# Moving the tail of a retention normalisation behind later attention units, on one core

## The reference, cut to what matters

```python
def retention_readout(y, g, gn_gain):
    mu = jnp.mean(y, axis=-1, keepdims=True)
    var = jnp.mean(jnp.square(y - mu), axis=-1, keepdims=True)
    y = (y - mu) * lax.rsqrt(var + EPS)
    y = jnp.swapaxes(y, 1, 2).reshape(y.shape[0], y.shape[2], -1) * gn_gain.astype(jnp.float32)
    return (y * jax.nn.silu(g.astype(jnp.float32))).astype(g.dtype)

def gated_merge(gates, ya, yb, yc, w_ret, w_win, w_na, w_out):
    ga, gb, gc = jnp.split(jax.nn.sigmoid(gates), N_BRANCHES, axis=-1)
    return (ga * (ya @ w_ret) + gb * (yb @ w_win) + gc * (yc @ w_na)) @ w_out
```

## Time and profile before

| what | value |
|---|---|
| median of 3 runs | 1686.57 us (1684.5 to 1687.13) |
| the profiled execution | 1686.03 us |
| its span, first to last instruction | 1684.2 us |
| TensorE matmul busy | 1439.9 us (85%) |
| VectorE busy | 807.2 us (48%) |
| ScalarE busy | 589.8 us (35%) |
| mean granted TensorE clock | 0.921 of full |

### The profile page before, as it was taken

The page is one execution under the profiler, slowest core; times in us unless marked ns, Lnnn a source line. Parts: engine busy times, 40 slices in busy tenths (PEclk is TensorE's granted clock), DMA queues, the critical chain, the costliest instruction groups (busy, mean ns, idle before and its releaser), DMA issues. The chain is left out here.

```text
span 1684.2 us, 26662 instructions
## 1 busy us (share of the span) xinstructions
PE 1439.9 (85%) x11126; PEld 1119.9 (66%) x11126; DVE 807.2 (48%) x1341; ACT 589.8 (35%) x844; POOL 25.3 (2%) x34
## 2 busy tenths in 40 slices
PE   5999998999967565566565699989999999999999
PEld 3889886578952121121121388549999999999999
DVE  4353337756641010100101378665777467787753
ACT  3432125775321101001010252564444365844331
POOL 1100000000000000000000000000000000300000
PEclk8999999999969787786887799999999999999999
DMA  9755447653668999999999945873455544445420
GB/s 396 298 229 219 151 182 293 232 193 111 248 242 343 428 427 429 426 429 427 428 427 428 415 175 186 327 269 126 178 177 190 184 169 182 167 162 191 182 101 26
DMA packets 48990, 437.68 MB, mean 260 GB/s; under 512 B 5232, under 2 KB 7664, under 8 KB 8304
## 3 DMA queue, kind: packets, MB, share of 16 engines
q1 hardware_dynamic: 47872, 430.99, 64.7%
q10 hardware_dynamic: 1008, 5.07, 0.7%
HBM read 434.99 MB, written 1.05 MB: 259 GB/s over the span
## 5 line engine op out<-in xcount | busy, mean ns | idle before, releaser
L788 PE MATMUL bank<-arena_r,ring_r 128*128 128x256 f32 (+1 forms) x5016 | 700.3, 285 | 12.4 <-DVE ring_end_r L1860 4.9
L788 PEld LDWEIGHTS bank<-arena_r,ring_r 128*128 128x128 f32 x5016 | 652.4, 191 | 28.0 <-issue 14.4
L1860 DVE TENSOR_TENSOR ring_r<-ring,ring_r 128x2048 fp32r<-128x2048 f32 (+1 forms) x108 | 246.0, 2280 | 153.7 <-ACT ring_r L1510 153.5
L1157 PE MATMUL bank<-ring,arena 128*32 128x512 f32 x1008 | 164.6, 789 | 123.5 <-DMA ring<-in_w 121.2
L1510 ACT ACTIVATE ring_r<-ring 128x2048 fp32r<-128x2048 f32 (+1 forms) x108 | 205.0, 1899 | 121.9 <-PE bank L788 114.6
L1157 PEld LDWEIGHTS bank<-ring,arena 128*32 128x32 f32 x1008 | 33.7, 127 | 242.7 <-DMA ring<-in_w 143.7
L788 PE MATMUL bank<-H_r,ring_r 128*128 128x256 f32 x816 | 183.6, 291 | 4.6 <-DVE H_r L1837 4.6
L788 PEld LDWEIGHTS bank<-H_r,ring_r 128*128 128x128 f32 x816 | 138.3, 198 | 7.9 <-issue 7.4
L2127 DVE TENSOR_TENSOR arena<-arena,bank 64x512 f32<-64x512 f32 x16 | 11.1, 691 | 272.7 <-ACT arena L1620 272.7
L1620 ACT ACTIVATE arena<-bank 64x512 f32<-64x512 f32 x16 | 9.4, 589 | 359.0 <-PE bank L1157 358.9
L788 PE MATMUL bank<-arena_r,ring_end_r 128*128 128x256 f32 (+1 forms) x400 | 114.8, 287 | 0.0
(11 more groups left out here) (284 smaller groups left out, 1483.3 us busy)
## 6 DMA issues: line engine op xcount, KB each, us to landing
ring<-in_w SPq DMA_DIRECT2D x93, 2048.0 KB, 25.7
ring<-in_w SPq DMA_DIRECT2D x171, 1024.0 KB, 4.9
ring_end<-in_w SPq DMA_DIRECT2D x45, 1024.0 KB, 4.9
ring<-in_bias ACTq DMA_DIRECT2D x1, 2048.0 KB, 12.3
ring_end<-in_w SPq DMA_DIRECT2D x1, 2048.0 KB, 23.6
H<-in_w SPq DMA_DIRECT2D x2, 1024.0 KB, 12.6
consts<-in_consts ACTq DMA_DIRECT2D x1, 1183.0 KB, 9.4
X<-in_x SPq DMA_DIRECT2D x1, 1024.0 KB, 5.5
```

The lines of the kernel that those rows point to most:

```text
L788: i = nc.tensor.matmul(o, lhsT, rhs, start=start, stop=stop, skip_group_check=grouped)
L1157: last = matmul(bank[0][32 * j:32 * j + 32, :], x_cur[:, k, :], columns(slot_of(c), j, 512), start=k == 0, stop=k == KT - 1)
L1860: v.tensor_tensor(r(lo), lo, r(hi), ALU.subtract).then_inc(lo_ready, 1)
```

## The change

Each head now has a tail step of its own, ("ret_fin", h), on VectorE. The four stand directly behind att_n(6), att_n(8), att_n(10) and att_n(12). The scaled variance and its square root are kept where the high part of y will lie (`y_r_hi`) in place of the spare tiles, since those also serve as probability buffers. TensorE's first branch product waits for four heads in place of two pairs. ScalarE's and TensorE's orders are otherwise as before, and no transfer is moved in the list.

```diff
+RET_UNITS = (6, 8, 10, 12)
...
             s.append(("att_n", i - LAG + 1))
+            if i - LAG + 1 in RET_UNITS:
+                s.append(("ret_fin", RET_UNITS.index(i - LAG + 1)))
...
-                    pe.wait_ge(ret_ready, 2)
+                    pe.wait_ge(ret_ready, R_HEADS)
...
-                f(rope_b if p else rope_a, rope_b if p else rope_a, ACT.Sqrt).then_inc(ret_std, 1)
+                f(y_r_hi[:, 2 * p:2 * p + 2, :], y_r_hi[:, 2 * p:2 * p + 2, :], ACT.Sqrt).then_inc(ret_std, 1)
...
             def step_ret_var(p):
-                t = rope_b if p else rope_a
+                t = y_r_hi[:, 2 * p:2 * p + 2, :]
                 b = job(("ret_var", p))
                 takes(v.tensor_scalar(t, two(b), 1.0 / P, EPS, ALU.mult, ALU.add), ("ret_var", p))
-                dve.wait_ge(ret_std, p + 1)
+
+            def step_ret_fin(h):
+
+                t, y = y_r_hi[:, h, :], y_r[:, h, :]
+                dve.wait_ge(ret_std, h // 2 + 1)
                 link(v.reciprocal(t, t))
-                y = y_r[:, 2 * p:2 * p + 2, :]
                 link(v.tensor_tensor(y, y, t, ALU.mult))
-                for h in (2 * p, 2 * p + 1):
-                    link(v.scalar_tensor_tensor(y_r[:, h, :], y_r[:, h, :], col("ret_gn", h), g_r[:, h, :], ALU.mult,
-                                                ALU.mult))
-                hi = y_r_hi[:, 2 * p:2 * p + 2, :]
-                link(v.tensor_copy(r(hi), y))
-                v.tensor_tensor(r(y), y, r(hi), ALU.subtract).then_inc(ret_ready, 1)
+                link(v.scalar_tensor_tensor(y, y, col("ret_gn", h), g_r[:, h, :], ALU.mult, ALU.mult))
+                link(v.tensor_copy(r(t), y))
+                v.tensor_tensor(r(y), y, r(t), ALU.subtract).then_inc(ret_ready, 1)
```

More of the change, by code:

```diff
@@ L2349, in _ @@
                      "rot": step_rot, "vr": values("vr", v_r), "vn": values("vn", v_n), "kvw": step_kvw, "kn": step_kn,
-                     "ret_s": step_ret_s, "ret_mean": step_ret_mean, "ret_var": step_ret_var, "att_s": step_att_s,
+                     "ret_s": step_ret_s, "ret_mean": step_ret_mean, "ret_var": step_ret_var, "att_s": step_att_s, "ret_fin": step_ret_fin,
                      "att_n": step_att_n, "att_o": step_att_o, "branch": step_branch, "mix_out": step_mix_out,
```

## The result

The changed kernel takes 1689.45 us (median of 17 runs, 1687.52 to 1693.68) where the kernel before, run on the same chip, takes 1685.27 (17 runs, 1682.01 to 1688.38). The ratio is 1.0027 with a 95% interval of 1.002 to 1.0034: slower by 4.2 us. The forecast was +5.2 us and 1691.2. The distance between the two times, 1.75 us, is made of two parts: 1.0 is the forecast of the change, and 0.76 its starting point, 1686.03, which lay above this median of the kernel before.

A forecast was written before the change was run, and what follows sets the result against it. Up to the branch at 401 us a serial VectorE-ScalarE chain, with TensorE from 316 to 356, was taken as the bound, then transfers. -7.44 + 12.05 + 0.6 = +5.2 us on 1686.03 gave 1691.2, range 1688.5 to 1693.5.

The forecast's parts named there:

- The gain: In front of the first attention unit: without the two pair tails VectorE starts unit 0 at its scores, 7.44 us earlier.
- I take 0: At gate 4: its weight chunk, needed at 276.1 us, lands in time; cost 0 to 0.4 us, taken as 0.
- Head 0: Before VectorE's unit 8: one head's tail of 3.44 us, partly absorbed by slack, leaves unit 9 late by 1.73 us.
- Heads 1 to 3: Before VectorE's units 10, 12 and 14: not hidden by idle time, 3.44 us each, 10.32 in all.
- The clock: At TensorE's gate 11: a longer idle gap drops the clock to half rate, 0 to 0.6 us, taken as 0.6.
- near 3.9 before gates 9, 10 and 11: TensorE's idle times before these gates grow by 3.44 us, to near 3.9 us.
- The sum at the branch: At the first branch product: -7.44 gained, 12.05 added by the heads, 0.6 for the clock, together +5.2 us.
- one for one: Behind the branch products at 401 us: what is won or lost before them reaches the end unchanged.
- A: Units 8 to 15: VectorE's idle time covers the heads and the 7.44 us lead stays, 1678.6 us; chance 0.12.
- B: Before 305 us: TensorE's clock comes back early, lead 9 to 10.6 us, about 1688 us; chance with mixes 0.15.
- C: Behind gate 11: the clock falls during the last turns and value products, up to 4.6 us more, 1695.8; chance 0.10.
- D: At unit 0: something else, such as a chunk, holds it, so only the cost stays, 1698.1 us; chance 0.03.

The follow-up runs named there:

- the early idle time: The changed kernel with its four heads put directly behind the maxima of units 0, 2, 4 and 6: 1678.51 us, 0.9965 of the kernel before.
- the tail left out: The kernel before without the retention tail's reciprocal, product, and gain and gate, high and low part kept: 1678.42 us, 0.9963 of the kernel before.
- gate 4's chunk first: The changed kernel with gate 4's chunk fetched in front of a modulation chunk: 1689.65 us, 1.0026 of the kernel before.

## Why the prediction was right

The sign, the mechanism and nearly the size were right; the change cost 4.2 us where 5.2 were forecast. Term by term:

- **The gain, forecast 7.44 us.** The reasoning held: the scores are next, and VectorE takes them up 1.17 us after TensorE's first product (forecast 1.16, from one place in the trace). TensorE starts gate 4 without idle time, 12.4 us after the scores (forecast 12.5). Lead and wait for the chunk add up to 7.3 to 7.4 us in every kernel that moves all four heads, and with no wait the lead was 7.43. What failed was the step "I take 0" for the chunk: it cost 1.35 us here, and 0.2 to 2.0 in the other executions; the bound of 0 to 0.4 was too narrow, because it rested on the median landing of 4.9 us where this transfer took 7.6, and 8.1 in the trace that the prediction was made from. The prediction looked in the right place and bounded it with the wrong row. The change itself showed leads of 5.97, 5.86 and 5.78 in three executions.
- **Head 0, forecast 1.73.** Measured: VectorE's unit 8 came 3.40 us late against the lead and unit 9 1.65. Two pieces of slack took the rest, as in the working: VectorE's idle time in front of split_lo(gate 8) fell from 4.26 to 3.36 us, so that step was 2.5 late, and TensorE's lateness at unit 9, 0.77 before, is gone. (The prediction writes 2.6 late; its own figures give 2.5, and 1.73 is 2.5 less 0.77.)
- **Heads 1 to 3, forecast 3.44 each.** The rounds grew by 3.26, 3.41 and 3.09. One head lasts 3.43 us; each of its five parts, priced from groups of the same shape, came out within 0.01. The small remainder, 0.56 us in all, was slack that the forecast left out; which wait gave it was not traced. Total with head 0: 11.41 for 12.05.
- **The clock, forecast 0.6.** Close to nothing was measured. The idle time around gate 9 did not stay in one piece: it was 2.34 us in front of att_t(8), whose turns and products paid for it (0.66), and 2.25 in front of the gate, which ran at full clock; before gate 11 it was 2.21. Gates 9 and 11 took 5.98 and 5.99 us. Only gate 10, behind 3.40 us in one piece, took 7.48, and the longer round hid that. The forecast's "near 3.9 before gates 9, 10 and 11" was wrong for this reason. With a longer head (5.77 us of idle time before gate 11) the term appeared, at 1.1 us.
- **The sum at the branch** was forecast as +5.2 and measured as +5.40 in the first execution, 5.50 and 5.63 in the two repeats: the gain 1.5 too large and the costs 1.2 too large, in opposite directions. That these two nearly cancel is luck and not accuracy.
- **From the branch to the end**, "one for one" held for the early idle time (-7.06 at the branch, -6.5 to -7.4 at the end of the same execution) but not quite here, where `mix_out` gave back 1.5 us at a better clock. The forecast had no term for that. Its cause is open.

The rivals. *A* (the idle time covers the heads) is refuted by the rounds of 15.6 to 16.2 us with unchanged idle time; what A describes is true of the place behind the maxima, 7 us faster. *B* (a lead beyond 7.44) is refuted by att_t(3): it comes 40.46 us after the scores (308.54 - 268.08), later than the forecast's 39.0 (308.7 - 269.71), and behind 0.60 us of waiting for VectorE. *C* (the clock falls in the tail) occurred neither in the change nor with the reciprocals tripled: there gate 11 itself was slow, and the tail behind it ran at full clock. *D* (unit 0 does not move) is refuted at once by the first add, although D's own example, a chunk, turned out to hold a part of it.

The Trainium skill, "TensorE: Matmul & The Clock Gate", in its table on why this matters for kernels, warns of long idle gaps. The runs here agree for 3.40 and 5.77 us of idle time, each followed by a slow gate, and for the kernel before's 3.94. They do not agree for the 3.44 us before gate 8 with the reciprocals tripled, behind which the clock was full. They also show gaps of 1.94 and 2.34 us followed by a clock of 0.61 and 0.66, and gaps of 2.21 and 2.25 us followed by full clock. The rule gave the direction; what a gap costs here had to come from rows.

## What to carry to other kernels

Idle time on an in-order engine has a near side and a far side: work put in front of the hand-over that the next engine waits for is paid in full and leaves the idle time as it was, the same work put right behind the hand-over is free as long as it fits into the idle time. So look for the instruction that *starts* the idle time (here the maxima), and put the work directly behind it; the share of idle time in a stretch says nothing. And when a stall is removed, bound what is late next by the landing of that very transfer in the trace (here 8.1 us) and not by the median of its group (4.9), and expect that taking the wait from one chunk can hand it to the next.

## What had not been expected of the hardware

- The wait for one and the same 1 MB chunk, issued in the same order, was 0.2 to 1.5 us in seven executions of kernels that move all four heads, 2.0 with the tail left out, and 0.25 and 1.4 in two executions of the same kernel. The transfer itself took 6.4 to 8.3 us in all these.
- The same 192 matmuls behind the same idle times of 1.26 and 0.81 us take 21.13 or 22.6 us, by a granted clock of 1.00 or 0.57 at their start, also within one kernel. A margin of 1.5 us either way therefore hangs on such a place, a third of what this change moves.
- Idle times of 1.94 and 2.34 us were followed by a low clock, 2.21 and 2.25 us were not, and nor were 3.44. It differs for one place as well: 2.25 us before gate 9 were followed by 1.00 in the change and by 0.53 with gate 4's chunk first. In front of att_t(3), 1.94 us were followed by 0.61 in one kernel, and 1.95 us by 1.00 in an execution of the kernel before, which lost nothing (131.09 us to the branch):

```profile
314.46 1.09 PE L792 MATMUL bank<-consts,ring 128*128 128x128 f32 x8 [1.95 <-DVE ring L2037]
...
314.00:318.00 4.00, 3.54 (x28) 1.58 (x28) 3.97 (x9) 0.17 (x1) 0.00 (x0) 1.00 0.01 4
```

What a gap costs could not be read from its length.
